# The sum of squares of ten norms: six of eight feature tiles added on GpSimd, the rest summed on TensorE

## The reference

```python
def rms_norm(x, g):
    xf = x.astype(jnp.float32)
    y = xf * lax.rsqrt(jnp.mean(xf * xf, axis=-1, keepdims=True) + EPS)
    return (y * g.astype(jnp.float32)).astype(x.dtype)

...
    for layer in range(DEPTH):
        need_ctx = layer < DEPTH - 1
...
        x = x + g1 * (mx @ w_out[layer])
        hx = modulate(rmsnorm(x, norm2_g[layer]), sh2, sc2)
        x = x + g2 * squared_relu_mlp_2(hx, w_mlp1[layer], w_mlp2[layer])
...
    return rmsnorm(x, final_g)
```

## Time and profile before

| | |
|---|---|
| time, median of 3 runs | 3822.45 us (3810.04 to 3832.63) |
| time of the profiled execution | 3806.64 us |
| its span, first to last instruction | 3804.9 us |
| busy: PE / DVE / ACT / POOL | 3585.1 / 1999.1 / 1231.8 / 135.8 us |
| TensorE clock granted over the span | 0.952 of full speed |

### The profile page before, as it was taken

The page is one execution under the profiler, slowest core; times in us unless marked ns, Lnnn a source line. Parts: engine busy times, 40 slices in busy tenths (PEclk is TensorE's granted clock), DMA queues, the critical chain, the costliest instruction groups (busy, mean ns, idle before and its releaser), DMA issues.

```text
span 3804.9 us, 42418 instructions
## 1 busy us (share of the span) xinstructions
PE 3585.1 (94%) x17568; PEld 2824.2 (74%) x17568; DVE 1999.1 (53%) x3717; ACT 1231.8 (32%) x2053; POOL 135.8 (4%) x242
## 2 busy tenths in 40 slices
PE   7999899999989999998999889999998998879998
PEld 6656678876867678887986557888886885558886
DVE  5564488856654478854136764323335236654434
ACT  5353343234453333333112222332233212134332
POOL 0200000001040000000000000000000000000000
PEclk9999999999999999999999859999999998789999
DMA  5302155522212145533210011212122320112331
GB/s 169 107 19 70 45 166 177 170 85 83 73 32 72 46 153 172 170 113 123 80 56 31 21 44 38 77 57 67 56 67 75 106 67 17 39 45 90 98 100 56
DMA packets 214108, 317.01 MB, mean 83 GB/s; under 512 B 5304, under 2 KB 162618, under 8 KB 212636
## 3 DMA queue, kind: packets, MB, share of 16 engines
q1 hardware_dynamic: 198108, 243.00, 19.7%
q0 software_dynamic: 15808, 71.31, 5.6%
HBM read 300.66 MB, written 14.49 MB: 83 GB/s over the span
## 4 chain that ended last, share of the span: by engine, by line
PE 83%; DVE 11%; ACT 3%; issue 2%; DMA 1%; POOL 0%; SPq 0%; DVEq 0%; POOLq 0%; ACTq 0%
PE ps L94 82%; DVE t L115 5%; ACT t L100 3%; DVE t L107 3%; PE ps L97 1%; DVE t L111 1%; DVE t L112 0%; DVE ps L107 0%; DVE ps L115 0%; DVE t L121 0%; DMA t<-gates_away 0%; DVE t L125 0%; DVE t L118 0%; DVE ps L112 0%; DMA t<-in_mem 0%
## 5 line engine op out<-in xcount | busy, mean ns | idle before, releaser
L94 PE MATMUL ps<-t,t 128*128 128x512 f32 (+7 forms) x17152 | 3530.7, 369 | 194.3 <-DVE t L107 97.6
L94 PEld LDWEIGHTS ps<-t,t 128*128 128x128 f32 (+3 forms) x17152 | 2774.2, 191 | 924.5 <-issue 200.8
L100 ACT ACTIVATE t<-t 128x1024 fp32r<-128x1024 f32 (+6 forms) x1168 | 830.9, 743 | 1278.4 <-PE ps L94 903.3
L107 DVE TENSOR_TENSOR t<-t,t 128x1024 fp32r<-128x1024 f32 (+5 forms) x882 | 763.6, 890 | 724.8 <-ACT t L100 709.3
L100 ACT ACTIVATE t<-ps 128x512 f32<-128x512 f32 (+5 forms) x490 | 248.4, 531 | 1051.8 <-PE ps L94 1022.9
L115 DVE SCALAR_TENSOR_TENSOR t<-t,t,t 128x256 f32<-128x256 f32 (+4 forms) x935 | 438.7, 530 | 7.7 <-ACT t L100 1.2
L107 DVE TENSOR_TENSOR t<-ps,t 128x512 f32<-128x512 f32 (+4 forms) x293 | 187.6, 660 | 266.6 <-PE ps L94 203.8
L115 DVE SCALAR_TENSOR_TENSOR t<-ps,t,t 128x512 f32<-128x512 f32 (+1 forms) x228 | 139.7, 661 | 301.5 <-PE ps L94 281.4
L118 DVE COPY t<-ps 128x256 f32<-128x256 f32 (+3 forms) x169 | 75.7, 477 | 270.8 <-PE ps L94 253.1
L100 ACT ACTIVATE t<-ps,t 128x512 f32<-128x512 f32 (+3 forms) x106 | 61.7, 582 | 133.1 <-PE ps L94 95.5
L111 DVE TENSOR_SCALAR t<-t,t 128x256 f32<-128x256 f32 (+3 forms) x257 | 93.8, 380 | 5.8
(11 more groups left out here) (31 smaller groups left out, 273.6 us busy)
## 6 DMA issues: line engine op xcount, KB each, us to landing
t<-in_w_ff SPq DMA_DIRECT2D x64, 1024.0 KB, 7.6
t<-in_w_mlp SPq DMA_DIRECT2D x64, 1024.0 KB, 5.5
t<-in_ada_w POOLq DMA_DIRECT2D x48, 1024.0 KB, 5.9
t<-in_w_in SPq DMA_DIRECT2D x30, 1024.0 KB, 5.2
t<-in_w_qkv_o SPq DMA_DIRECT2D x12, 1024.0 KB, 5.2
t<-in_w_mem_kv SPq DMA_DIRECT2D x8, 1024.0 KB, 6.4
t<-in_w_mem_q SPq DMA_DIRECT2D x8, 1024.0 KB, 5.1
t<-in_w_mem_o SPq DMA_DIRECT2D x8, 1024.0 KB, 5.2
```

What stands on the lines that cost most here:

```text
L94: return Issued(self, self.e and self.e.matmul(o, l, r, start=start, stop=stop, skip_group_check=True))
L100: return Issued(self, self.e and self.e.activation(o, i, f, **kw))
L107: return Issued(self, self.e and self.e.tensor_tensor(o, a, b, op))
```

## The change

For the ten norms GpSimd now adds up the squares. ACT writes the square of tile 0 into RS, which is free until the norm's logarithm, and those of tiles 1 to 7 into the two buffers by turns. GpSimd adds tiles 1 to 5 to RS, one instruction each (`add_squares`). TensorE takes no ones product between the pairs any more: after the last pair, `last_sums` takes one over RS, one over the square of tile 6 and one over that of tile 7. The square of tile k (from 3 on) now waits for GpSimd's addition of tile k-2, which also covers tile 7, and the product over RS waits for the addition of tile 5.

```diff
+        def last_sums(key, segs):
+
+            for s, n in enumerate(segs):
+                opening(6 + s)
+                pe.wait_ge("added", (key, s), 5)
+                pe.matmul(P[6 + s][:, 0:n], cst("ones"), RS[s][:, 0:n], True, False)
+            for s, n in enumerate(segs):
+                for k in (6, 7):
+                    pe.wait_ge("square", (key, s), k)
+                    pe.matmul(P[6 + s][:, 0:n], cst("ones"), (SQ, TMP)[s][k % 2][:, 0:n], False, k == 7).then_inc("sumsq", (key, s), k)
+                free[6 + s] = [("rs", (key, s))]
...
         def project_out(us, x, ready_k, key, segs):
 
-            for b, u in enumerate(us):
+            for u in us:
                 feature(u, x, ready_k)
-                if b > 0:
-                    for si, n in enumerate(segs):
-                        square_sum((key, si), 6 + si, n, two(b - 1), (SQ, TMP)[si])
-            for si, n in enumerate(segs):
-                square_sum((key, si), 6 + si, n, two(3), (SQ, TMP)[si])
+            last_sums(key, segs)
...
-                for b, u in enumerate(f2[j]):
-
-                    def sums(y):
-                        k = 4 * b + 2 * y
-                        if k > 0:
-                            for si, n in enumerate(segs):
-                                square_sum((key, si), 6 + si, n, [k - 2, k - 1], (SQ, TMP)[si])
-
-                    feature(u, tiles.HID[j % 2], lambda kk: [("hidden", key, j, kk, si) for si in range(len(segs))],
-                            sums if j == 7 else None)
+                for u in f2[j]:
+                    feature(u, tiles.HID[j % 2], lambda kk: [("hidden", key, j, kk, si) for si in range(len(segs))])
                     modulate()
-            for si, n in enumerate(segs):
-                square_sum((key, si), 6 + si, n, [6, 7], (SQ, TMP)[si])
+            last_sums(key, segs)
...
+        def square_of(key, s, src, n, k, after):
+
+            if k == 0:
+                act.wait_ge(*rs_free[s])
+                o = RS[s]
+            else:
+                o = (SQ, TMP)[s][k % 2]
+                if k > 2:
+                    act.wait_ge("added", (key, s), k - 2)
+                elif s == 0:
+                    act.wait_ge(*sq_free[k % 2])
+            act.wait_ge(*after)
+            act.activation(o[:, 0:n], src[:, k, :], ACT.Square).then_inc("square", (key, s), k)
+            if k == 0:
+                rs_free[s] = ("added", (key, s), 5)
+            elif s == 0 and k > 5:
+                sq_free[k % 2] = ("sumsq", (key, s), k)
...
     def gpsimd(pl):
+        def add_squares(key, segs):
+
+            for k in range(1, 6):
+                for s, n in enumerate(segs):
+                    if k == 1:
+                        pl.wait_ge("square", (key, s), 0)
+                    else:
+                        pl.wait_ge("added", (key, s), k - 1)
+                    pl.wait_ge("square", (key, s), k)
+                    pl.tensor_tensor(RS[s][:, 0:n], RS[s][:, 0:n], (SQ, TMP)[s][k % 2][:, 0:n], ALU.add).then_inc(
+                        "added", (key, s), k)
...
+            add_squares(f"xat{l}", [S])
+            add_squares(f"ff{l}", [S])
             pl.wait_ge("nlo", f"ff{l}", 7, 0)
...
+            add_squares("mix1" if l == 0 else "n1_0", [S])
...
+            add_squares(f"n2_{l}", [n for _, n in segs])
+            add_squares("n1_1" if l == 0 else "fin", [n for _, n in segs])
```

More of the change, by code:

```diff
@@ L570, in weights, with feature @@
             return [hl[:, a, :].rearrange("p (k n) -> p k n", k=u.kc) for a in range(2)]
-        def feature(u, x, ready_k, between=None):
+        def feature(u, x, ready_k):
             wv = weights(u)
-            for y, pair in enumerate(u.pairs):
+            for pair in u.pairs:
                 for kk in range(u.kc):
@@ L590, in feature @@
                         free[v.bank] = ([] if v.opens else free[v.bank]) + [("ev", u.n, t.m, z)]
-                if between is not None:
-                    between(y)
         def tokens(u, x, ready_k):
@@ L1305, in project_out @@
                     for s, (dst, n) in enumerate(streams):
-                        squares_of((key, s), (SQ, TMP)[s], dst, n, [m], lambda k: ("ev", u.n, k, s))
+                        square_of(key, s, dst, n, m, ("ev", u.n, m, s))
         def feed_forward(ff, tiles, nkey, key, segs, streams):
@@ L1342, in feed_forward @@
                             for s, (dst, n) in enumerate(streams):
-                                if s == 1 and m < 2:
-                                    act.wait_ge(*tmp_free[m])
-                                squares_of((key, s), (SQ, TMP)[s], dst, n, [m], lambda k: ("ev", u.n, k, s))
+                                if s == 1 and m in (1, 2):
+                                    act.wait_ge(*tmp_free[m % 2])
+                                square_of(key, s, dst, n, m, ("ev", u.n, m, s))
         act.wait_ge("mem_in")
```

## The result

The changed kernel takes 3763.64 us (median of four runs, 3762.3 to 3764.54), the kernel before 3816.24 us (four runs, 3808.1 to 3832.63). The ratio is 0.9854, 95% interval 0.9827 to 0.9882: faster by 1.5%. Forecast were 3776 us and a saving of 44.9 us. The two profiled executions differ by 3806.64 - 3764.54 = 42.1 us.

What follows compares the result with a forecast made beforehand. TensorE was taken to bound the kernel (PE busy 94%). 37.8 us between the pairs plus 7.1 in the tails, additions at 0, gave 44.9 us off 3822.45, 3777.6; it said 3776 us, own range 3760 to 3795, outer ends 3753 and 3807.

Steps and rivals of the forecast that it cites:

- Part 1: Between the pairs in all ten norms: the ones products of tiles 0 to 3 leave TensorE's path, saving 37.8 us.
- Rival A: Between the pairs: the sums were covered anyway, only the tails gain, 7.1 us, giving 3815 us; chance 4%.
- The tails: Behind each norm's last pair: squares and products of tiles 6 and 7 start earlier, saving 7.1 us in all.
- for n1_0 ...: 0, and this wait is the cover: Tail of n1_0: TensorE waits for the context until 1740.08 in both kernels, so the gain there is 0.
- rival C: Norm tails: thinner TensorE list lets the clock fall, remaining products cost 26 us more in all, 3803 us; chance 3%.
- The additions: On GpSimd: 1.3 us per 128x512 addition (upper end 2.14), 0.75 us per 128x256, ending in time.
- Cost 0: GpSimd's additions and the waits for them cost 0, hidden by the matmuls of the last pair.
- Rival D: GpSimd's serial RS chain does not keep up; at 6 us per addition the time is 3845 us; chance 3%.
- the formula: RS chain: last addition ends 2.0 + 5a us behind the first eviction, a being one addition's time with its waits.
- The shared access: GpSimd additions beside DVE subtractions with two SBUF operands: both stretch, but subtractions have 4.8 us to spare; cost 0.
- the 1.03 of the estimate: DVE subtractions meeting GpSimd additions: 1.03 us more for each addition, from 4.42 us against 2.36 for two subtractions.
- The range's lower end of 3753: Whole kernel: lowest time forecast, if all 47.3 us are saved and the runs are fast like the profiled one.

Runs made afterwards that it cites:

- e4: The changed kernel with the same additions on DVE instead of GpSimd, ahead of the next pair's eviction; 3763.97 us, ratio 0.9871.
- e7: The changed kernel with the change kept only in the four feed-forward norms; projection norms keep their ones products between the pairs; 3800.58 us, ratio 0.9971.
- e10: The changed kernel with the first norm, mix0, treated too: eight squares summed on GpSimd, one product instead of eight; 3764.94 us, ratio 0.9878.
- e9: The changed kernel with two more 512-column products over constants in n1_0's tail alone, ahead of the wait for the context; 3771.5 us, ratio 0.9896.
- e5: The changed kernel with GpSimd's sum ending at tile 3; tiles 4 to 7 keep their own products in the tail; 3786.47 us, ratio 0.993.
- e8: The changed kernel with 58 more products over constants behind the norms' last products, keeping TensorE busy in the tails; 3754.7 us, ratio 0.9847.
- e11: The changed kernel with mix0's squares also summed on GpSimd and the extra products over constants in the norms' tails; 3752.15 us, ratio 0.9841.
- e1: The changed kernel without GpSimd's 60 additions, waits for them replaced by waits for the square; 3763.92 us, ratio 0.9877.
- e3: The changed kernel with four further GpSimd additions per addition, in the eight norms of one token group; 3840.79 us, ratio 1.0071.
- e2: The changed kernel with two further GpSimd additions per addition, in the eight norms of one token group; 3778.8 us, ratio 0.9902.
- e6: The changed kernel with GpSimd adding tiles 1 to 7 and TensorE taking one product, over RS; 3787.17 us, ratio 0.993.

## Why the prediction was right, and where it was off

**The bound.** That TensorE's list sets the pace, and a product is worth its length, held at every place: 11.20, 5.60, 8.48 and, at n2_0, 16.96 us between the evictions, so Part 1 is 37.8 us as forecast. (The prediction reckoned the room for two groups at 8.48 us in both places; n2_0 has twice that, which hurts nothing.) e4 shows that the shorter list of TensorE pays, whichever engine adds. e7 shows it from the other side: where the products stay, so does their time. Rival A (covered sums) is out for the ten norms, and true of the eleventh, which the change left alone (e10).

**The tails.** The mechanism was right: squares of tiles 6 and 7 released by DVE, the RS product out of the way. The size was not: -5.0 instead of -7.1 us. In the nine ordinary tails the term was 0.07 to 0.08 too large each. The logarithm came 3.50 instead of 3.41 us behind the eviction. The step that failed is "for n1_0 ...: 0, and this wait is the cover": the wait covers the products, but with fewer products TensorE stands idle in it for longer (2.22 us instead of the 1.38 of the earlier trace rows), its clock fell, and 16 transposes took 3.54 instead of 2.05 us. e9 shows the cause: with two products in the gap they take 2.05 again, as in e5, e8 and e11. It is rival C in one of ten norms, at 1.36 us.

**The additions.** 1.3 us each was right: the groups by line give 1321 ns as the mean of all 58 in after, eight of which were there before; the 50 new ones have a mean of 1296:

```profile
L107 POOL TENSOR_TENSOR t<-t,t 128x512 f32<-128x512 f32 x58 | 76.6, 1321 | 1723.5 <-ACT t L100 1721.6
```

The ten of 128x256, put at 0.75 us, took 1.13 on average (0.73 to 1.72). Cost 0 was right as well (e1, e4). Rival D's mechanism is real: e3 turns the gain into a loss, as the chain says, though its 3840.79 us met the forecast of 3842 by errors that cancel. e2 adds what the formula lacked: a wait in a tail costs its length and then the lower clock for the products behind it.

**The shared access.** The subtractions beside additions took 3.3 us instead of 2.36 (1706.51 above), 0.95 more for a pair with about one addition beside it, near the 1.03 of the estimate. That pair began 1.09 us before the second of two additions ended (1707.60), and those two took 2.68 us, hardly more than alone: here only DVE was held up. It costs nothing in the ten norms, as forecast (e1), though the prediction read the rule on the shared ports as one against any work on GpSimd: DVE has room there; it did reach the path in e10. The Trainium skill, page "SBUF — State Buffer", section "SBUF: two separate sides", names such DVE operations as those that meet GpSimd at the shared ports; the trace agrees, with these 3.3 us.

**The absolute number.** 3776 us was 12 us too high, though the saving was 2.8 us too large. I had started from 3822.45, the median of three runs. Later runs of the kernel before, 37 in all, lie in two groups: 27 at 3803.55 to 3809.82 us with a granted clock of 0.951 to 0.953, and ten at 3819.54 to 3835.84 with 0.943 to 0.950. The median of three happened to be of the upper group. From the median of the eleven runs beside e9 to e11 it is 3808.9 - 44.9 = 3764.0 us. That this meets the measured 3763.64 so closely is luck, since the sum of the places was 2.1 us too large. The range's lower end of 3753 doesn't come out of its own terms either: 3806.64 - 47.3 is 3759.3.

**The two lengths.** The gap between the groups, some 13 us, is also the gap between the profiles in the stage from n1_0 to n2_0: 590.4 to 590.6 us in after, e1, e3, e4 and e6; 603.9 to 604.0 in e2, e5 and e9; 592.2 to 593.7 in e8, e10 and e11. Without their 5.14 us of products, before's profile has 594.3 and e7's 606.8. Of the others none changes a matmul in it, except e8 and e11, which put seven more at its start. The stage ahead of xat1 varies too, from 303.9 to 312.8 us. The granted clock differs, as the stretches of e9 show. What decides which length a kernel gets is open: e9 differs from after by two products some 8 us ahead of the stage, e5 by tails that are 1.6 us longer. The clock of the transposes just ahead doesn't decide it, for 16 transposes took 1.99 us in e3 and 2.05 in e9. No run sets the length on purpose. That before's own two groups are of this stage is likely by their size and by their granted clocks; the runs of the upper one left no profile.

Each kernel has one profile and 4 to 10 runs, and after's four runs stand beside four of before only, while before's median beside the others was 3807.62 to 3808.91. So differences of a few microseconds between medians show little; what is said of places rests on the stages and tails in the profiles.

## What to carry to other kernels

When TensorE bounds a kernel, moving a reduction's products onto an idle engine is worth their full length where matmuls of the same block hide the additions, and worth less than nothing in the tail, where no work is left to hide them: sum all but the last tiles elsewhere, and leave those to TensorE. Count the room of each place (here 5.6 us a pair against 1.3 us an addition) and look for the shortest unit, since that is where a stretched neighbour shows. And compare variants by stage, not only by total: a difference of 13 us here lay in a stage that no variant touched, and went with a lower granted clock there.

## What the runs showed of the hardware that was not expected

- More work on TensorE made the kernel faster. 58 products over constants in idle places (e8) took 8.9 us off, where the matmuls behind them ran at 2.4 GHz instead of 1.2 (granted 1.00 and 0.53 behind ff1). It paid where TensorE set the pace of the restart, and not where DVE did (n1_1).
- A wait of the same length (3.55 us, e6) ended with a full-speed product in one norm and with one at half speed in another. The same tail is worth 6.2 or 7.1 us.
- The same holds between two kernels whose lists are the same up to that point: 96 matmuls behind a wait of 3.04 us took 13.10 us in e10 (granted clock 0.87) and 11.57 in e11 (1.00).
- The same program has executions 13 us apart. A kernel with two products more (e9: six runs, 3769.75 to 3775.0) was profiled with the long form of a stage that after has in its short form; that the two products did it isn't shown.
- Two SBUF-to-SBUF subtractions of DVE take 2.36 us alone, 3.3 with about one GpSimd addition beside them, and the additions 1.3 us alone, 2.1 beside such subtractions (4.23 for two in e10).
